# First MLP of a two-layer decoder: the relu turned by VectorE blocks and ScalarE quarter copies, modulation pieces issued on GpSimd's queue

## The chip, the core and the metric

The kernel runs on one core of a Trainium2 chip. The metric is device time in microseconds (us), lower is better. Besides the queues for transfers the core has TensorE (PE in the rows; PEld are its weight loads), VectorE (DVE), ScalarE (ACT), GpSimd (POOL) and SyncE (SP), which here only issues transfers. Each engine carries out its own instructions strictly in their order and waits on semaphores in that order.

## What is computed

Two decoder layers over 256 tokens with 2048 features, in float32. Cut to what matters here:

```python
for i in range(DEPTH):                      # 2 layers
    mod = (c_act @ w_ada[i] + b_ada[i])[:, None, :]
    sh_a, sc_a, g_a, sh_m, sc_m, g_m = jnp.split(mod, N_MOD, axis=-1)
    h = x * (1.0 + sc_a) + sh_a
    y = (diff_attention, sliding_window_attention)[i](h, ...)
    x = layer_norm(ALPHA * x + (1.0 + g_a) * y, ln_mix_g[i], ln_mix_b[i])
    h = x * (1.0 + sc_m) + sh_m
    y = jnp.square(jax.nn.relu(h @ w_up[i])) @ w_down[i]        # 2048 -> 8192 -> 2048
    x = layer_norm(ALPHA * x + (1.0 + g_m) * y, ln_mlp_g[i], ln_mlp_b[i])
```

The change concerns the squared-relu MLP of the first layer, and the loading of those parts of `w_ada` (the modulation weights) that are summed while this MLP runs.

## The kernel before

**Blocks.** Every large product is cut into blocks of 2048 input features by 512 output columns. A block's weights are four quarters of 1 MB (`raw`, five slots), each of two subtiles of 128x1024. ScalarE copies a subtile to `w_hi` in a shorter float format (`split_hi`, L528, six slots), VectorE subtracts (`split_lo`, L901) and writes the rest, `w_lo`, over `raw`. TensorE multiplies a subtile in twelve matmuls of 512 columns (L1709 to L1711): high by high, low by high, high by low, for two feature tiles and two token halves. So a block is 8 subtiles and 96 matmuls. ScalarE may be six subtiles ahead of TensorE, since `split_hi` waits for the slot (`used`).

**An MLP** has four rounds of eight blocks: four up blocks, each 512 columns of `h @ w_up`, then four down blocks, which multiply the 2048 squared columns by `w_down` and add to `y`. The loops over `b` in `mlp` are one block behind: at loop index b the engines split block b+1 and handle the result of block b between the subtiles (`before`, `later`, `hooks`; the number of a hook is the subtile after which it runs). With `i = b % 8`, the result is that of an up block for i from 0 to 3 and of a down block for i from 4 to 6. The text calls the block in which the result of an up block is handled a *turning block*; there are 16 in each MLP.

**Turning.** The result of an up block has tokens in partitions, and the down product needs features there. In the first layer ScalarE takes the relu out of PSUM into `R` (L553) after subtile 1 of the turning block, TensorE turns it by eight 128x128 transposes against the identity (`turn_up`, L1603) into PSUM, ScalarE squares it twice from there, once exactly and once into `f_hi` (L560, L561), and VectorE subtracts (`up_lo`, L1031) and gives `f_lo`. In the second layer (`ON_CHIP = (1,)`) TensorE takes no part: VectorE turns 16 pieces of 32x256 from SBUF to SBUF (L1040), which also moves each to its partitions, and ScalarE squares from there (L572, L573).

**Modulation pieces.** Beside this VectorE sums `c * w_ada` over 16 pieces of 128x1024 (512 KB) at a time (`ada_tile`, L929; the first of 16 is L926) in `ada_w`, which has four slots. In the first MLP these are 192 pieces, six or seven in each of the first 28 blocks, placed by `MLP_ADA` after subtiles 0, 1, 3, 5, 6, 7 and, where there are seven, 4. When 16 are summed, TensorE turns the sum (L1627, eight transposes) and VectorE reduces it (L960) after subtile 6. In the first four turning blocks VectorE also carries out the affine part of the layer norm (L1311, L1312) after subtile 7.

**Queues.** SP issues the transfers of weights and pieces in one written order: a quarter, then the pieces that belong to it. Each quarter waits until TensorE has used the one five before it, each piece until VectorE has added the one four before it. GpSimd clears `y` before the MLP (L1581) and has a few tiny power operations for the norms.

Of the kernel before, what the change touches and what calls it, by code (L numbers as in the profile page):

```python
# [21 lines left out]
KT = D // P  # L22
# [35 lines left out]

ON_CHIP = (1,)

# [43 lines left out]
UNIT_AT_B = {8 * (50 + i) + 3 + k: 8 * i + k for i in range(NCH) for k in range(8)}  # L104
MLP_HALVES = (12, 2)
MLP_GATE = (8, 0)
READY = 6
# [40 lines left out]
def trunk(nc, x_in, c_in, w_ada, b_ada, ln_mix_g, ln_mix_b, ln_mlp_g, ln_mlp_b, w_up, w_down,  # L148
          a_w_qkv, a_w_o, a_lambda_q1, a_lambda_k1, a_lambda_q2, a_lambda_k2, a_subln_g,
          b_w_qkv, b_b_qkv, b_sinks, b_w_o, b_b_o, ident_in, mask_in, rope_a_in, rope_b_in, out):  # L150
    with ExitStack() as ctx:
# [124 lines left out]
        ada_arrived = [sem(f"ada_arrived{i}") for i in range(ADA_SLOTS)]  # L276
        pre_arrived = [sem(f"pre_arrived{i}") for i in range(PRE_SLOTS)]
        ada_added = sem("ada_added")
        piece_taken = sem("piece_taken")
# [86 lines left out]
        def _(sp):  # L366
# [114 lines left out]
            def mlp(layer):  # L481
                def up(f, j):
                    col = f * D + j * NC
                    return lambda q: w_rows(w_up[layer], q * 4 * P, col)

                def down(f, j):
                    return lambda q: w_rows(w_down[layer], f * D + q * 4 * P, j * NC)

                load_block(up(0, 0))
                parts = [(1, 0), (1, 1), (1, 3), (1, 4), (0, 5), (1, 2)] if layer == 0 else [(1, 5)]  # L490
                tiles = iter([ada_src(l, part, half, kt) for l, part in parts for half in range(2) for kt in range(KT)])

                def of():
                    return next(tiles)

                for b in range(8 * QUARTERS - 1):
                    it, i = b // 8, b % 8
                    src = up(it, i + 1) if i < 3 else down(it, i - 3) if i < 7 else up(it + 1, 0)
                    load_block(src, mlp_pieces(b, 2 * len(parts)), of)

            mlp(0)

            for j in (4, 0, 1, 2, 3):
# [15 lines left out]
        def _(act):  # L519
# [35 lines left out]
            def up_square(j):  # L555

                def run():
                    act.wait_ge(t_full[0], st.t0.at(1))
                    wait(act, f_ready, st.up.at())
                    act.activation(SQ.rearrange("p t n -> p (t n)"), turn[:, 0], ACT.Square)  # L560
                    act.activation(f_hi[:, 4 * j:4 * j + 4], T[0], ACT.Square).then_inc(t_free[0], 1)  # L561
                    st.t0.n += 1
                    st.up.n += 1
                return run

# [229 lines left out]
            def mlp(layer, site, base):  # L795
# [3 lines left out]
                for b in range(8 * QUARTERS - 1):  # L799
# [5 lines left out]
                    if layer == 1 and b == 8 * QUARTERS - 3:  # L805
                        hk[0] = load_last_rows
                    if layer in ON_CHIP:
                        if i < 4:
                            hk[5] = up_square_there(i)
                        block_(before=up_relu if i < 4 else None, hooks=hk, at=2)  # L810
                        continue
# [75 lines left out]
        def _(dve):  # L887
# [31 lines left out]
            def ada_tile():  # L919
# [3 lines left out]
                src = ada_w[:, a.n % ADA_SLOTS]  # L923
                dve.wait_ge(ada_arrived[a.n % ADA_SLOTS], a.at(1 - PRE // ADA_SLOTS, 16, over=ADA_SLOTS))
                if kt == 0:
# [101 lines left out]
            def up_lo(i):  # L1027

                def run():
# [3 lines left out]
                    st.t0.n += 1  # L1033
                return run

            def up_turn_half(first):
# [417 lines left out]
            def mlp(layer, site, g):  # L1454
# [5 lines left out]
                for b in range(8 * QUARTERS - 1):  # L1460
# [11 lines left out]
                    if layer in ON_CHIP and i < 4:  # L1472
                        hooks[3] = up_turn_rest
                        block_(before=up_turn_across, later=(5, up_rest(i)), ada=mlp_pieces(b, halves), hooks=hooks)
                        continue
# [75 lines left out]
        def _(pool):  # L1551
# [21 lines left out]
            for u in range(UNITS_A):  # L1573
# [4 lines left out]
                power(sm[:, 7, 0:1], sm[:, 7, 1:2], orstd_ready)  # L1578
            site(1)
            pool.wait_ge(h_ready, 28)  # L1580
            pool.memset(y[:], 0.0).then_inc(y_clear, 1)  # L1581
            site(2)

# [527 lines left out]
```

## Time and profile before

| | us |
|---|---|
| median of 3 runs | 2228.59 |
| lowest and highest | 2226.88, 2228.90 |
| the profiled execution itself | 2228.67 |
| its span, first to last instruction | 2226.9 |

The profiled execution is within 0.1 us of the median, and 1.8 us of it lie outside the span. The mean granted clock of TensorE is 0.993 of full speed. In the rows below a time stands in us from the start of the span; a group of instructions has the number of them as xN, and the square bracket behind a row gives the idle time of the engine just before it and what ended that. Busy time of TensorE is modelled, and neighbouring matmuls overlap, so what an instruction costs there is read from the distance between starts.

### The profile page before, as it was taken

What the parts mean: (1) busy time and instruction counts of PE and PEld (TensorE: products, weight loads), DVE (VectorE), ACT (ScalarE), POOL (GpSimd) and SP (SyncE); (2) the same over time, 40 slices, a digit from 0 to 9 for tenths busy, and PEclk for the clock granted to TensorE, in tenths of its full rate; (3) what the DMA queues carried; (4) which work ended last, traced back from release to release, by engine and by line L of the source; (5) the groups of instructions that cost most, each with busy time, mean ns of one, the idle gap of its engine ahead of it and who ended that gap; (6) DMA issues with size and microseconds to landing.
All of it is one profiled execution on the core that took longest, in us unless ns stands there. A gap on an engine that the chain in (4) does not pass through costs nothing.

```text
span 2226.9 us, 26022 instructions
## 1 busy us (share of the span) xinstructions
PE 2168.5 (97%) x9952; PEld 1791.8 (80%) x9952; DVE 1790.6 (80%) x2057; ACT 981.3 (44%) x1330; POOL 33.4 (2%) x53
## 2 busy tenths in 40 slices
PE   6999999999999999999999999999999999999997
PEld 6887888877888888888888788777888888888886
DVE  6899998887997897888786888777966865874877
ACT  1135444546433443443353655536534443443441
POOL 0001000000000000000000000000000000000000
PEclk9899999999999999999999999999999999999999
DMA  9999888877999999999985643365766676666663
GB/s 360 384 331 347 322 320 300 306 245 256 361 364 325 354 366 335 325 380 350 323 311 190 198 152 119 122 207 190 236 221 223 213 241 206 219 217 219 228 234 113
DMA packets 262592, 596.41 MB, mean 268 GB/s; under 512 B 13426, under 2 KB 14788, under 8 KB 262468
## 3 DMA queue, kind: packets, MB, share of 16 engines
q1 hardware_dynamic: 254800, 579.45, 74.2%
q10 hardware_dynamic: 7668, 15.30, 2.2%
q8 instruction: 79, 1.29, 0.2%
q14 instruction: 45, 0.37, 0.0%
HBM read 592.60 MB, written 2.10 MB: 267 GB/s over the span
## 4 chain that ended last, share of the span: by engine, by line
PE 88%; DVE 7%; DMA 1%; issue 1%; ACT 1%; SPq 0%; DVEq 0%; POOL 0%; ACTq 0%; POOLq 0%
PE pair L1709 25%; PE pair L1711 25%; PE pair L1710 25%; DVE acc L916 2%; DVE w_lo L901 1%; PE pair L1967 1%; PE pair L1969 1%; PE pair L1968 1%; PE pair L1729 1%; PE pair L1731 1%; PE pair L1730 1%; PE turn L2041 1%; DMA y<-in_w_ada_dram 1%; PE turn L2022 1%; PE turn L1603 1%
## 5 line engine op out<-in xcount | busy, mean ns | idle before, releaser
L528 ACT ACTIVATE w_hi<-raw 128x1024 fp32r<-128x1024 f32 x712 | 726.8, 1056 | 620.2 <-PE pair L1711 297.4
L901 DVE TENSOR_TENSOR w_lo<-raw,w_hi 128x1024 fp32r<-128x1024 f32 x712 | 852.5, 1220 | 117.0 <-ACT w_hi L528 110.8
L1709 PE MATMUL pair<-w_hi,h_hi 128*128 128x512 f32 x1456 | 581.3, 399 | 1.5 <-DVE w_lo L901 0.8
L1711 PE MATMUL pair<-w_hi,h_lo 128*128 128x512 f32 x1456 | 567.8, 390 | 0.0
L1710 PE MATMUL pair<-w_lo,h_hi 128*128 128x512 f32 x1456 | 567.3, 390 | 0.0
L1709 PE MATMUL pair<-w_hi,f_hi 128*128 128x512 f32 x1056 | 414.0, 392 | 0.1
L1711 PE MATMUL pair<-w_hi,f_lo 128*128 128x512 f32 x1056 | 411.1, 389 | 0.0
L1710 PE MATMUL pair<-w_lo,f_hi 128*128 128x512 f32 x1056 | 410.9, 389 | 0.0
L929 DVE SCALAR_TENSOR_TENSOR acc<-ada_w,cvec,acc 128x1024 f32<-128x1024 f32 x300 | 383.6, 1279 | 1.8 <-DVE x L1312 0.9
L1709 PEld LDWEIGHTS pair<-w_hi,h_hi 128*128 128x128 f32 x1456 | 273.5, 188 | 62.9 <-DVE w_lo L901 6.3
L1711 PEld LDWEIGHTS pair<-w_hi,h_lo 128*128 128x128 f32 x1456 | 273.2, 188 | 58.4
L1710 PEld LDWEIGHTS pair<-w_lo,h_hi 128*128 128x128 f32 x1456 | 273.7, 188 | 55.5 <-issue 1.2
L1709 PEld LDWEIGHTS pair<-w_hi,f_hi 128*128 128x128 f32 x1056 | 198.2, 188 | 43.7 <-DVE w_lo L901 2.1
L1710 PEld LDWEIGHTS pair<-w_lo,f_hi 128*128 128x128 f32 x1056 | 198.3, 188 | 41.7 <-issue 1.0
L1711 PEld LDWEIGHTS pair<-w_hi,f_lo 128*128 128x128 f32 x1056 | 198.2, 188 | 41.5
L1040 DVE STREAM_TRANSPOSE work<-work 32x256 f32<-32x256 f32 x256 | 111.6, 436 | 55.7 <-ACT work L553 52.2
L553 ACT ACTIVATE work<-pair 128x1024 f32<-128x1024 f32 x32 | 32.9, 1029 | 222.3 <-PE pair L1711 222.3
L1066 DVE TENSOR_TENSOR y<-pair,y 128x1024 f32<-128x1024 f32 x30 | 36.7, 1224 | 101.2 <-PE pair L1711 101.2
L572 ACT ACTIVATE work<-work 128x1024 f32<-128x1024 f32 x16 | 17.0, 1062 | 90.7 <-DVE work L1040 90.7
L1967 PE MATMUL pair<-w_hi,f_hi 128*128 128x512 f32 x128 | 53.6, 419 | 1.9 <-DVE f_lo L1513 1.9
L1969 PE MATMUL pair<-w_hi,f_lo 128*128 128x512 f32 x128 | 50.1, 391 | 0.0
L1968 PE MATMUL pair<-w_lo,f_hi 128*128 128x512 f32 x128 | 49.9, 390 | 0.0
(190 smaller groups left out, 1669.5 us busy)
## 6 DMA issues: line engine op xcount, KB each, us to landing
ada_w<-in_w_ada_dram SPq DMA_DIRECT2D x320, 512.0 KB, 6.1
raw<-in_w_up_dram SPq DMA_DIRECT2D x128, 1024.0 KB, 6.1
raw<-in_w_down_dram SPq DMA_DIRECT2D x128, 1024.0 KB, 5.2
raw<-in_a_w_qkv_dram SPq DMA_DIRECT2D x48, 1024.0 KB, 7.6
ada_f<-in_w_ada_dram SPq DMA_DIRECT2D x44, 512.0 KB, 11.5
raw<-in_b_w_qkv_dram SPq DMA_DIRECT2D x20, 1024.0 KB, 5.2
raw<-in_a_w_o_dram SPq DMA_DIRECT2D x16, 1024.0 KB, 6.5
raw<-in_b_w_o_dram SPq DMA_DIRECT2D x16, 1024.0 KB, 5.1
```

What stands on the lines that cost most here:

```text
L528: act.activation(w_hi[:, (b.n * SUB + n) % SPLITS], raw[:, slot, k:k + 2], ACT.Copy).then_inc(hi_ready, 1)
L901: dve.tensor_tensor(w_lo[:, slot, k:k + 2], raw[:, slot, k:k + 2], w_hi[:, (b.n * SUB + n) % SPLITS].bitcast(F32), ALU.subtract).then_inc( ...
L916: ins = dve.scalar_tensor_tensor(dst, src, cvec[:, n % KT:n % KT + 1], dst, ALU.mult, ALU.add)
L929: ins = dve.scalar_tensor_tensor(acc[:, half], src, cvec[:, kt:kt + 1], acc[:, half], ALU.mult, ALU.add)
L1040: ins = dve.transpose(by_token(rows32(up_rows(RR), c), a), by_feature(rows32(up_rows(R), a), c))
L1066: dve.tensor_tensor(cols(y, j), pair[:, pp], cols(y, j), ALU.add).then_inc(evacuated, 1)
L1709: pe.matmul(o, hi[:, kt, at], w[:, k], start=kt == 0, stop=False)
L1710: pe.matmul(o, hi[:, kt, at], wl[:, k], start=False, stop=False)
L1711: mm = pe.matmul(o, lo[:, kt, at], w[:, k], start=False, stop=kt == KT - 1)
L1967: pe.matmul(o, f_hi[:, kt, at], w[:, k], start=kt == 0, stop=False)
L1968: pe.matmul(o, f_hi[:, kt, at], wl[:, k], start=False, stop=False)
L1969: mm = pe.matmul(o, f_lo[:, kt, at], w[:, k], start=False, stop=kt == KT - 1)
```

## The change

Four things change, all for the first MLP.

1. `ON_CHIP` becomes `(0, 1)` and `BY_SCALAR = (0,)` is added. TensorE no longer turns the relu of the first MLP. VectorE turns all of `R` in one instruction of 128x1024 in blocks of 32x32 into PSUM (`up_turn`), and ScalarE moves the blocks to their partitions by 16 copies of 32x256 out of PSUM into `RR` (`up_move`), eight after subtile 3 and eight after subtile 4 of the turning block.
2. The two squares come after subtile 5 and read `RR` in SBUF; the relu is taken after subtile 2 in place of 1; `f_lo` is made after subtile 5 in place of 4.
3. The 192 pieces of the first MLP are no longer issued by SP but by GpSimd, in a loop of its own, each with the same wait for the piece four before it. The first four are issued before `y` is cleared.
4. The pieces of that stretch have semaphores of their own (`pool_arrived`), and `ada_tile` picks which to wait for.

```diff
-ON_CHIP = (1,)
+ON_CHIP = (0, 1)
+BY_SCALAR = (0,)
+POOL_PIECES = MLP_HALVES[0] * KT
@@ SyncE
-                parts = [(1, 0), (1, 1), (1, 3), (1, 4), (0, 5), (1, 2)] if layer == 0 else [(1, 5)]
+                tiles = iter([ada_src(1, 5, half, kt) for half in range(2) for kt in range(KT)])
-                    load_block(src, mlp_pieces(b, 2 * len(parts)), of)
+                    load_block(src, mlp_pieces(b, MLP_HALVES[layer]) if layer == 1 else (), of)
@@ ScalarE
+            def up_move(first, last):
+                def run():
+                    act.wait_ge(up_blocks, st.turned.n + 1)
+                    for i in range(first, last):
+                        a, c = i // 4, i % 4
+                        ins = act.activation(by_token(rows32(up_rows(RR), c), a),
+                                             by_feature(rows32(turn[:, 0], a), c), ACT.Copy)
+                    if last == 16:
+                        ins.then_inc(up_moved, 1)
+                return run
@@ ScalarE, mlp
                     if layer in ON_CHIP:
+                        if i < 4 and layer in BY_SCALAR:
+                            hk[3], hk[4] = up_move(0, 8), up_move(8, 16)
@@ VectorE
+            def up_turn(b, pp):
+                dve.wait_ge(evacuated, b + 3)
+                dve.transpose(turn[:, 0], up_rows(R)).then_inc(up_blocks, 1)
@@ VectorE, mlp
-                        hooks[3] = up_turn_rest
-                        block_(before=up_turn_across, later=(5, up_rest(i)), ada=mlp_pieces(b, halves), hooks=hooks)
+                        if layer not in BY_SCALAR:
+                            hooks[3] = up_turn_rest
+                        block_(before=up_turn if layer in BY_SCALAR else up_turn_across, later=(5, up_rest(i)), ada=mlp_pieces(b, halves), hooks=hooks)
@@ GpSimd
             site(1)
+            def load_ada(n):
+                a = st.ada
+                for _ in range(n):
+                    pool.wait_ge(ada_added, a.at(1))
+                    pool.dma_start(ada_w[:, a.n % ADA_SLOTS], next(tiles)).then_inc(pool_arrived[a.n % ADA_SLOTS], 16)
+                    a.n += 1
+            load_ada(ADA_SLOTS)
             pool.wait_ge(h_ready, 28)
             pool.memset(y[:], 0.0).then_inc(y_clear, 1)
+            load_ada(POOL_PIECES - ADA_SLOTS)
             site(2)
```

ScalarE's queue in the first turning block of the first MLP, before (work is R, RR and the third of these buffers):

```order
L553 ACTIVATE work<-pair 128x1024
L528 ACTIVATE w_hi<-raw 128x1024 x3
L560 ACTIVATE work<-turn 128x1024
L561 ACTIVATE f_hi<-turn 128x1024
L528 ACTIVATE w_hi<-raw 128x1024 x5
```

The same place in the changed kernel:

```order
L556 ACTIVATE work<-pair 128x1024
L531 ACTIVATE w_hi<-raw 128x1024
L575 ACTIVATE work<-turn 32x2x4x32 x8
L531 ACTIVATE w_hi<-raw 128x1024
L575 ACTIVATE work<-turn 32x2x4x32 x8
L531 ACTIVATE w_hi<-raw 128x1024
L587 ACTIVATE work<-work 128x1024
L588 ACTIVATE f_hi<-work 128x1024
```

Between the relu and the squares there are now three splits with 16 copies between them, where there were three splits alone.

VectorE's queue from subtile 2 of a turning block in the second round, before:

```order
L901 TENSOR_TENSOR w_lo<-raw,w_hi 128x1024 x2
L929 SCALAR_TENSOR_TENSOR acc<-ada_w,cvec,acc 128x1024
L901 TENSOR_TENSOR w_lo<-raw,w_hi 128x1024
L1031 TENSOR_TENSOR f_lo<-work,f_hi 128x1024
L929 SCALAR_TENSOR_TENSOR acc<-ada_w,cvec,acc 128x1024
```

The same place in the changed kernel:

```order
L918 TENSOR_TENSOR w_lo<-raw,w_hi 128x1024
L1063 STREAM_TRANSPOSE turn<-work 128x1024
L918 TENSOR_TENSOR w_lo<-raw,w_hi 128x1024
L953 SCALAR_TENSOR_TENSOR acc<-ada_w,cvec,acc 128x1024
L918 TENSOR_TENSOR w_lo<-raw,w_hi 128x1024
L953 SCALAR_TENSOR_TENSOR acc<-ada_w,cvec,acc 128x1024
L918 TENSOR_TENSOR w_lo<-raw,w_hi 128x1024
L1086 TENSOR_TENSOR f_lo<-work,f_hi 128x1024
```

The transpose is new, between subtiles 2 and 3, and `f_lo` stands one subtile later.

GpSimd's queue from the norm ahead of the first MLP, before:

```order
L1561 TENSOR_TENSOR rstd<-rstd,minus_half 128x1 x2
L1581 MEMSET y 128x4096
L1561 TENSOR_TENSOR rstd<-rstd,minus_half 128x1 x2
L1586 MEMSET y 64x1024 x2
L1561 TENSOR_TENSOR rstd<-rstd,minus_half 128x1 x2
```

The same place in the changed kernel:

```order
L1591 TENSOR_TENSOR rstd<-rstd,minus_half 128x1 x2
L1619 DMA ada_w<-in_w_ada_dram 128x1024 x4
L1624 MEMSET y 128x4096
L1619 DMA ada_w<-in_w_ada_dram 128x1024 x188
L1591 TENSOR_TENSOR rstd<-rstd,minus_half 128x1 x2
```

The 192 transfers stand ahead of and behind the clearing of `y`; the power operations of the next norm come behind all of them.

## Rows read from the trace of the kernel before

**Rows 1.** The page: busy time and share of TensorE; chain by engine

```profile
PE 2168.5 (97%) x9952; PEld 1791.8 (80%) x9952; DVE 1790.6 (80%) x2057; ACT 981.3 (44%) x1330; POOL 33.4 (2%) x53
PE 88%; DVE 7%; DMA 1%; issue 1%; ACT 1%; SPq 0%; DVEq 0%; POOL 0%; ACTq 0%; POOLq 0%
```

**Rows 2.** Busy by stretch: PE, PEld, DVE, ACT, POOL, clock, DMA share, GB/s

```profile
524.00:1158.00 634.00, 634.00 (x2887) 525.37 (x2886) 535.72 (x470) 271.92 (x275) 0.00 (x0) 1.00 0.95 344
640.00:662.00 22.00, 22.00 (x103) 18.28 (x102) 20.94 (x20) 9.64 (x10) 0.00 (x0) 1.00 1.04 397
```

**Rows 3.** Timeline of TensorE around one turn: start, us, instruction

```profile
709.35 0.40 PE L1711 MATMUL pair<-w_hi,h_lo 128*128 128x512 f32 x1
709.58 1.04 PE L1603 MATMUL turn<-ident,work 128*128 128x128 f32 x8
710.38 0.47 PE L1709 MATMUL pair<-w_hi,h_hi 128*128 128x512 f32 x1
710.69 0.39 PE L1710 MATMUL pair<-w_lo,h_hi 128*128 128x512 f32 x1
```

**Rows 4.** Timeline of VectorE: two down blocks' results, each released by TensorE

```profile
659.92 1.22 DVE L1066 TENSOR_TENSOR y<-pair,y 128x1024 f32<-128x1024 f32 x1 [1.02 <-PE pair L1711]
...
681.68 1.23 DVE L1066 TENSOR_TENSOR y<-pair,y 128x1024 f32<-128x1024 f32 x1 [2.16 <-PE pair L1711]
```

**Rows 5.** Waits in the first MLP, 524 to 1158: us in all, times, longest

```profile
DVE w_lo L901 <- ACT w_hi L528: 47.4, 19, 6.8
ACT work L560 <- PE turn L1603: 37.4, 16, 2.5
DVE f_lo L1031 <- ACT f_hi L561: 25.2, 16, 1.6
```

**Rows 6.** Timeline of ScalarE at the start of a turning block

```profile
704.33 1.03 ACT L553 ACTIVATE work<-pair 128x1024 f32<-128x1024 f32 x1 [9.76 <-PE pair L1711]
705.26 2.94 ACT L528 ACTIVATE w_hi<-raw 128x1024 fp32r<-128x1024 f32 x3
```

**Rows 7.** Timeline of VectorE in the same block

```profile
712.63 1.23 DVE L1031 TENSOR_TENSOR f_lo<-work,f_hi 128x1024 fp32r<-128x1024 f32 x1 [1.60 <-ACT f_hi L561]
713.77 1.28 DVE L929 SCALAR_TENSOR_TENSOR acc<-ada_w,cvec,acc 128x1024 f32<-128x1024 f32 x1
714.97 1.22 DVE L901 TENSOR_TENSOR w_lo<-raw,w_hi 128x1024 fp32r<-128x1024 f32 x1
716.11 1.28 DVE L929 SCALAR_TENSOR_TENSOR acc<-ada_w,cvec,acc 128x1024 f32<-128x1024 f32 x1
```

**Rows 8.** Timeline of VectorE, second layer's turning by 32x256 pieces

```profile
1751.23 3.58 DVE L1040 STREAM_TRANSPOSE work<-work 32x256 f32<-32x256 f32 x8 [3.23 <-ACT work L553]
1754.82 1.23 DVE L901 TENSOR_TENSOR w_lo<-raw,w_hi 128x1024 fp32r<-128x1024 f32 x1
1756.08 3.59 DVE L1040 STREAM_TRANSPOSE work<-work 32x256 f32<-32x256 f32 x8
```

**Rows 9.** Timeline of ScalarE, second layer's attention: small copies out of PSUM

```profile
1306.89 0.38 ACT L855 ACTIVATE work<-turn 128x256 f32<-128x256 f32 x1 [0.94 <-PE turn L2031]
1307.17 0.37 ACT L860 ACTIVATE f_hi<-turn 64x256 fp32r<-64x256 f32 x1
1307.44 1.05 ACT L528 ACTIVATE w_hi<-raw 128x1024 fp32r<-128x1024 f32 x1
```

**Rows 10.** Timeline of ScalarE, second layer: the squares from SBUF

```profile
1781.77 1.06 ACT L572 ACTIVATE work<-work 128x1024 f32<-128x1024 f32 x1 [5.67 <-DVE work L1040]
...
1783.68 2.94 ACT L528 ACTIVATE w_hi<-raw 128x1024 fp32r<-128x1024 f32 x3
```

**Rows 11.** Timeline of VectorE: the affine part after subtile 7, first round

```profile
585.15 1.21 DVE L1311 TENSOR_TENSOR x<-x,bc 128x1024 f32<-128x1024 f32 x1
...
587.83 1.28 DVE L929 SCALAR_TENSOR_TENSOR acc<-ada_w,cvec,acc 128x1024 f32<-128x1024 f32 x1 [0.21 <-DVE x L1312]
```

**Rows 12.** The issues of pieces by SP (L374): time to landing

```profile
DMA to landing us min/median/max: 3.4/6.1/14.3
```

**Rows 13.** Groups of VectorE in the first MLP, 524 to 1158: busy us, mean ns

```profile
L960 DVE TENSOR_REDUCE mod<-turn 128x8 f32<-128x1024 f32 x8 | 9.8, 1220 | 1.8 <-PE turn L1627 1.8
L926 DVE TENSOR_SCALAR acc<-ada_w,cvec 128x1024 f32<-128x1024 f32 x11 | 8.2, 749 | 0.0
```

More of the change, by code:

```diff
@@ L277, in trunk @@
         pre_arrived = [sem(f"pre_arrived{i}") for i in range(PRE_SLOTS)]
+        pool_arrived = [sem(f"pool_arrived{i}") for i in range(ADA_SLOTS)]
         ada_added = sem("ada_added")
@@ L489, in mlp @@
                 load_block(up(0, 0))
-                parts = [(1, 0), (1, 1), (1, 3), (1, 4), (0, 5), (1, 2)] if layer == 0 else [(1, 5)]
-                tiles = iter([ada_src(l, part, half, kt) for l, part in parts for half in range(2) for kt in range(KT)])
+                tiles = iter([ada_src(1, 5, half, kt) for half in range(2) for kt in range(KT)])
                 def of():
@@ L498, in mlp @@
                     src = up(it, i + 1) if i < 3 else down(it, i - 3) if i < 7 else up(it + 1, 0)
-                    load_block(src, mlp_pieces(b, 2 * len(parts)), of)
+                    load_block(src, mlp_pieces(b, MLP_HALVES[layer]) if layer == 1 else (), of)
             mlp(0)
+            st.ada.n += POOL_PIECES
             for j in (4, 0, 1, 2, 3):
@@ L923, in ada_tile @@
                 src = ada_w[:, a.n % ADA_SLOTS]
-                dve.wait_ge(ada_arrived[a.n % ADA_SLOTS], a.at(1 - PRE // ADA_SLOTS, 16, over=ADA_SLOTS))
+                turns = (a.n - PRE) // ADA_SLOTS + 1
+                before = 3 * 2 * KT // ADA_SLOTS
+                if turns <= before:
+                    dve.wait_ge(ada_arrived[a.n % ADA_SLOTS], 16 * turns)
+                elif turns <= before + POOL_PIECES // ADA_SLOTS:
+                    dve.wait_ge(pool_arrived[a.n % ADA_SLOTS], 16 * (turns - before))
+                else:
+                    dve.wait_ge(ada_arrived[a.n % ADA_SLOTS], 16 * (turns - POOL_PIECES // ADA_SLOTS))
                 if kt == 0:
@@ L1579, in _ @@
             site(1)
+            parts = [(1, 0), (1, 1), (1, 3), (1, 4), (0, 5), (1, 2)]
+            tiles = iter([ada_src(l, part, half, kt) for l, part in parts for half in range(2) for kt in range(KT)])
+            st.ada.n = PRE + 3 * 2 * KT
+            def load_ada(n):
[5 more added lines that the diff above has]
+            load_ada(ADA_SLOTS)
             pool.wait_ge(h_ready, 28)
             pool.memset(y[:], 0.0).then_inc(y_clear, 1)
+            load_ada(POOL_PIECES - ADA_SLOTS)
             site(2)
```

## Prediction

> **What bounds the kernel now.** I read the page first: TensorE is busy for 97% of the span and holds 88% of the chain that ended last [rows 1]. Then the stretch of the first MLP, 524 to 1158 us: TensorE is busy for all 634 us of it at full clock, while VectorE is busy for 535.7 (84%), ScalarE for 271.9 (43%), and the transfer queues for 0.95 of their time at 344 GB/s [rows 2]. So there TensorE alone sets the pace, and whatever leaves its queue is won, as long as nobody else falls behind. The second thing to see is how little is free beside it: in one stretch of this MLP the transfers run at 397 GB/s with a share of 1.04 and VectorE is busy for 20.9 of 22 us [rows 2]. Last I read the waits. VectorE's own in this MLP are 47.4 us for ScalarE's splits and 25.2 us, 1.6 in each of 16 blocks, for the squares [rows 5]: that is its reserve, and it stands at fixed places in its queue.
>
> **What is removed.** A matmul of 512 columns follows the next at 0.227 us: the distance of two down results without any turn is 681.68 − 659.92 = 21.76 us for 96 of them [rows 4]. Around a turn the starts go 709.35, then 710.38 and 710.69 [rows 3]; that is 1.34 us for two steps of 0.227, so a turn costs 0.89. Sixteen go: **−14.2 us**. This is the whole possible gain, for the other work of TensorE stays.
>
> **What ScalarE gets.** A 128x256 copy from PSUM is followed by the next instruction after 0.28 us, a 64x256 copy after 0.27 [rows 9]. The change's copies have 256 elements in 32 partitions; I take 0.28, the row with the same type and an SBUF target. Eight are 2.24 us, 16 are 4.5. With eight splits at 0.945 (2.94 for three that overlap by their ends, [rows 6]), the relu (0.93, same rows) and the two squares (1783.68 − 1781.77 = 1.91, [rows 10]) ScalarE has 14.9 of 21.76 us: it fits by load. What counts is the latency from relu to squares.
>
> **What VectorE gets.** Sixteen transposes of 128x1024 into PSUM are not in the trace. From below: 32x256 takes 3.58/8 = 0.45 us [rows 8], so four times the columns cost at least what a subtraction of 128x1024 does, 1.22. From above: if the time went with partitions too, the 16 pieces of 32x256, 7.2 us. I take 1.24: 0.45 plus 768 more columns at the rate of VectorE's other operations (1.04 ns a column, from 1.22 us for 1024 against 0.45 for 256). Such a transpose doesn't overlap with its neighbours: the split ahead of it takes 1.26 instead of 1.14 (1754.82 to 1756.08, [rows 8]). So 1.36 us more in VectorE's queue in each turning block.
>
> **The new loop.** I carry one turning block on. Let X be the start of VectorE's transpose. It ends at X+1.24; with 0.04 for the semaphore ScalarE copies until 3.52, splits subtile 4 until 4.47, copies until 6.71, splits subtile 5 until 7.66, squares until 9.57 (its last end 9.67). VectorE idles for this (it has splits 4 and 5 and two pieces in the meantime) and then does f_lo (1.14, [rows 7]), a piece (1.20) and split 6 (1.14): the split ends at X+13.3. Four pairs of piece and split (2.34 each, [rows 7]) lead to the next transpose, at X+22.6. TensorE's block is 21.76. **The loop through both engines is 0.84 us longer than TensorE's block**, where before each block began afresh at TensorE's turn, which both engines waited for [rows 5].
>
> At the start of a round X is 1.26 us after TensorE's end of the up block: 0.20 to the relu, which lasts 1.03 [rows 6], and 0.03. TensorE wants subtile 6 at 6×2.72 = 16.3, split 6 ends at 14.5: 1.75 of reserve. A round has three such steps to the fourth turning block: 3×0.84 − 1.75 = 0.8 us of stall. A mod sum after subtile 6 costs VectorE 1.35 (1.22 [rows 13] and a small operation) and TensorE 0.89, so 0.46 more where it falls in a turning block before the last. For rounds 2, 3 and 4: 1.3 + 0.8 + 0.7 = **2.8 us**. In the down blocks VectorE wins back some 3 us a block.
>
> The first round has the affine part too: 587.83 − 585.15 = 2.68 us in each of four blocks [rows 11]. The loop is 25.3, 3.5 over TensorE's 21.76. Before, TensorE just escaped, since the turn gave VectorE 0.89 more and the loop was shorter by the copies and the transpose. Now the stalls are 3.5 − 1.75 = 1.8 in the second block, 3.5 and 3.5 in the third and fourth, and about 2.3 in the first down block, for the fourth affine part: **11.1 us**.
>
> Sum: −14.2 + 2.8 + 11.1 = −0.3 us. With copies at 0.265 the same working gives some 10.5 us of stalls, so −3.7; I put the forecast between the two rows, at −1.5. From the profiled execution's 2228.67: 2227.2, and since that is 0.1 from the median, **2227 us**. Copies at 0.30 give +5, at 0.35 +18, a transpose 0.1 longer +1.8 (each microsecond in the loop counts in some 14 of 16 blocks).
>
> **The pieces.** SP loses 192 issues, and its quarters no longer stand behind a piece's wait. That is worth nothing to TensorE, which never waited in this MLP; it gives ScalarE its weights earlier. GpSimd issues a piece when the one four before it has been added. In a dense run (after 6, 7, 0, 1) VectorE is back at that slot after three pairs and a split, 3×2.34 + 1.14 = 8.2 us; the landing takes 6.1 us in the median and up to 14.3 when it is queued behind quarters [rows 12]. In a queue of its own it stands behind no quarter, but shares the engines. Bounds: 0 if it stays under 8.2, and what one rival below gives if not. The memset of `y` isn't late: the four issues before it wait for pieces added before the norm. The power operations for the next norm stand behind the last piece, which is added three blocks before they are needed. Beside this SP's and ScalarE's queues are unchanged but for the order shown.
>
> VectorE's L926, at 749 ns against 1.28 us for any other piece of the same size, is in a faster form [rows 7, 13]. The Trainium skill, "SBUF — State Buffer" (the box on the DVE blocks DMA trap), says that a transfer issued from GpSimd has its descriptors written by that engine's cores, which are locked out while VectorE runs in a two-port fast mode, and tells one to issue from SP or ACT. By that rule at most 12 issues of 192 could meet an L926, 0.75 us each, inside the reserve of 2.1 us; the sum stays as it is. No row here shows an issue from GpSimd.
>
> **Rivals.**
> *The loop is shorter than I think (faster).* It decides at 0.23 us a copy, where the loop is down to TensorE's 21.76 and only the first round stalls. The bare columns of a copy are 0.22 us (0.945 for 1024 columns less 0.28 for 256, [rows 6, 9], is 0.87 ns each); at that the first round has 2.5 over, so 2.5 − 1.75, 2.5, 2.5 and 2.2, 8 us, and the time is 2222. If moreover VectorE didn't stop for ScalarE there, its load alone would count: 8×1.14 + 6.9×1.20 + 1.36 + 1.14 + 2.68 = 22.5, only 0.8 over 21.76, 3 us in four blocks, and 2217. Against: the small copies of [rows 9] have a fixed part, and [rows 5] show that VectorE does stop at the squares.
> *Pieces land late (slower).* It decides at 8.2 us from the slot's release. VectorE stands before the piece, and behind it in its queue are the splits TensorE needs. At 9 us the wait of 0.8 enters the loop about once a turning block, with half of it again elsewhere: some +7, so 2234; at 10 us +15 to +17, so 2243. For: the queues are at 0.95 already, and the turning blocks now ask for the same bytes in 21.76 us instead of 22.65. Against: the median of 6.1.
> The Trainium skill, "DMA: Bandwidth & Descriptors" (Specifications), gives about 1 us to the first byte from GpSimd's path and 0.6 from the other. By that the landing would be at 6.5, an estimate from that page and the median, still under the limit.
> *Quarter copies cost more (slower).* Their access is in runs of 32 elements with a stride. It decides at 0.29 us a copy; at 0.30 to 0.35 the time is 2233 to 2246. For: no such form is in the trace. Against: VectorE's pieces with the same pattern run at the usual rate [rows 8].
> *The change doesn't do what it says.* If TensorE's block stayed at 22.65 because something else needs that long (the transfers: 7.8 MB in 21.76 us are 358 GB/s), no stall and no gain: 2229. The 397 GB/s of [rows 2] speak against it.
>
> **How the numbers follow.** The loop as worked out, 2223 to 2231: 0.45, the likeliest, 2227. Shorter loop, 2217 to 2222: 0.14. Late pieces, 2232 to 2245: 0.20. Slow copies, 2233 to 2246: 0.14. Transfers as the bound, 2229: 0.07. A difference under 0.2%, 4.5 us, can't be told from none. Faster by more: 0.14 and 0.08 of the first case, 0.22. Slower by more: 0.34 and 0.01 of the first, 0.35. Within: 0.43. The range takes in the bounds of the copy's and the landing's cost and part of the short loop: 2219 to 2245.
>
> **What would show it.** TensorE without L1603, and blocks of 21.76 us in the later rounds; gaps of TensorE that end at VectorE's w_lo, 10 us or more in the first four turning blocks and about 1 us in each later round; the copies at 0.28 and the transpose at 1.24. ScalarE waiting for the transpose 0.3 us in the first turning block of a round and for longer in each next one. VectorE waiting for pieces before L953 would show the second rival; copies over 0.29 the third; stalls of 8 us or less in the first round, with the copies under 0.23, the first rival. I am wrong if the time is outside 2223 to 2231, and wrong in the mechanism if the stalls aren't mostly in the first round.

## The result and the profile after

| | before | after |
|---|---|---|
| median of three runs, us | 2228.59 | 2256.65 |
| lowest and highest, us | 2226.88, 2228.90 | 2255.18, 2257.93 |
| the profiled execution's span, us | 2226.9 | 2253.4 |

The changed kernel takes 1.0129 of the time of the kernel before (95% interval 1.0114 to 1.0143): 28.1 us more. The forecast was 2227 us with a range up to 2245, so it was wrong in size, and the change is a clear loss where I had given the largest chance, 0.43, to no difference. This section reads where the time went; the experiments then name the cause.

The page first, busy time by engine and the chain that ended last by engine; these answer to [rows 1]:

```profile
PE 2162.2 (96%) x9824; PEld 1772.6 (79%) x9824; DVE 1810.1 (80%) x2073; ACT 1081.2 (48%) x1586; POOL 137.1 (6%) x245
PE 71%; DVE 15%; ACT 7%; issue 6%; DMA 1%; SPq 0%; ACTq 0%; POOL 0%; DVEq 0%; POOLq 0%
```

TensorE has 128 instructions less, as it should, but its part of the chain fell from 88% to 71%, and VectorE (15%), ScalarE (7%) and the time that the profile can't name (issue, 6%) took it. Something other than TensorE sets the pace in a part of the program. Which part, the stretches tell. Each row below is one round's four turning blocks in the kernel after, from the first matmul of the first block to the first matmul of the down block behind them (columns as in [rows 2]):

```profile
521.80:628.64 106.84, 92.03 (x393) 71.71 (x391) 86.21 (x76) 70.01 (x111) 14.03 (x26) 1.00 0.86 296
717.64:814.13 96.49, 90.30 (x393) 72.24 (x392) 77.15 (x68) 68.95 (x110) 14.06 (x27) 1.00 0.91 320
902.99:999.87 96.88, 91.21 (x402) 73.06 (x401) 77.49 (x69) 68.97 (x110) 14.02 (x26) 1.00 0.92 327
1088.67:1184.70 96.03, 90.63 (x390) 72.38 (x388) 77.05 (x66) 68.98 (x110) 11.86 (x22) 1.00 0.87 306
```

And the same stretches of the kernel before:

```profile
523.70:615.27 91.57, 91.57 (x425) 76.22 (x424) 81.69 (x72) 44.75 (x46) 0.00 (x0) 1.00 0.93 331
704.13:795.74 91.61, 91.61 (x425) 76.22 (x424) 75.97 (x67) 44.63 (x46) 0.00 (x0) 1.00 0.91 326
884.60:977.10 92.50, 92.50 (x433) 77.05 (x432) 76.31 (x68) 44.74 (x46) 0.00 (x0) 1.00 0.95 339
1065.91:1158.36 92.45, 92.45 (x422) 76.14 (x421) 74.53 (x64) 45.84 (x47) 0.00 (x0) 1.00 0.91 324
```

The four rounds are 15.3, 4.9, 4.4 and 3.6 us longer, 28.1 in all, and the down blocks behind them are as long as before but for 0.1. So the whole loss sits in the sixteen blocks that the change touches, and more than half of it in the first round. (The profiled spans differ by 26.5 only, since this execution enters the stretch at 521.80 in place of 523.70. That start also lies at 524.66 in run 1 and at 523.35 in run 8 below; why is not shown.) TensorE runs at the full granted clock (1.00) in all of them; it only stands still: 92.03 busy of 106.84. The transfers' share fell to 0.86 to 0.92: they aren't the brake.

Who made TensorE wait? The waits of the kernel after in the same MLP, 524 to 1190 us (in all, times, longest):

```profile
DVE w_lo L918 <- ACT w_hi L531: 62.9, 33, 3.0
PEld pair L1753 <- DVE w_lo L918: 47.0, 36, 2.8
ACT work L575 <- DVE turn L1063: 42.1, 16, 5.4
PE pair L1753 <- DVE w_lo L918: 31.8, 29, 2.4
DVE f_lo L1086 <- ACT f_hi L588: 10.7, 16, 0.7
```

TensorE waits 29 times for VectorE's low parts of the weights, where it waited not once before. VectorE waits for ScalarE's high parts 33 times, twice in each of the sixteen blocks and once more. And ScalarE waits for VectorE's transpose (longest 5.4). It is the loop through both engines that the prediction had drawn, and it is longer than the prediction made it. ScalarE's timeline in one turning block shows by what:

```profile
720.20 3.07 ACT L575 ACTIVATE work<-turn 32x256 f32<-32x256 f32 x8 [0.38 <-DVE turn L1063]
723.28 1.06 ACT L531 ACTIVATE w_hi<-raw 128x1024 fp32r<-128x1024 f32 x1
724.36 3.10 ACT L575 ACTIVATE work<-turn 32x256 f32<-32x256 f32 x8
727.49 1.06 ACT L531 ACTIVATE w_hi<-raw 128x1024 fp32r<-128x1024 f32 x1
```

Eight copies last from 720.20 to 723.28, 0.385 us each from start to start, where [rows 9] gave 0.28. And the group of all of them on the page:

```profile
L575 ACT ACTIVATE work<-turn 32x256 f32<-32x256 f32 x256 | 96.1, 375 | 45.1 <-DVE turn L1063 42.1
```

A copy alone takes 375 ns, as the 128x256 copy of [rows 9] does with its 0.38. What is missing is the overlap: there the next instruction starts 0.1 us before the copy's end, here only after it. VectorE's timeline in the same block and at the start of the next:

```profile
718.90 1.26 DVE L1063 STREAM_TRANSPOSE turn<-work 128x1024 f32<-128x1024 f32 x1 [3.92 <-ACT work L556]
720.07 1.20 DVE L918 TENSOR_TENSOR w_lo<-raw,w_hi 128x1024 fp32r<-128x1024 f32 x1
...
724.37 1.22 DVE L918 TENSOR_TENSOR w_lo<-raw,w_hi 128x1024 fp32r<-128x1024 f32 x1 [1.92 <-ACT w_hi L531]
...
728.58 1.23 DVE L918 TENSOR_TENSOR w_lo<-raw,w_hi 128x1024 fp32r<-128x1024 f32 x1 [1.79 <-ACT w_hi L531]
730.47 1.23 DVE L1086 TENSOR_TENSOR f_lo<-work,f_hi 128x1024 fp32r<-128x1024 f32 x1 [0.67 <-ACT f_hi L588]
...
742.14 1.22 DVE L918 TENSOR_TENSOR w_lo<-raw,w_hi 128x1024 fp32r<-128x1024 f32 x1
743.28 1.25 DVE L1063 STREAM_TRANSPOSE turn<-work 128x1024 f32<-128x1024 f32 x1
```

From transpose to transpose 743.28 − 718.90 = 24.4 us, where the prediction had 22.6 and TensorE's block is 21.76. Behind each group of eight copies stands a split that VectorE waits for. Last the pieces on GpSimd: their issues and the time from issue to landing.

```profile
L1619 POOL DMA_DIRECT2D ada_w<-in_w_ada_dram x192 | 103.7, 540 | 549.2 <-DVE acc L953 529.0
DMA to landing us min/median/max: 3.8/6.5/9.0
```

### The profile page after: what moved, and what is told of

The parts are those of the page before. It is cut to its first block, busy times and chain, and to the rows that moved or that the text cites. A ratio compares the mean times of both kernels' runs of the same rounds, so it can differ in the third digit from the quotient of the medians.

```text
span 2253.4 us, 26022 instructions
## 1 busy us (share of the span) xinstructions
PE 2162.2 (96%) x9824; PEld 1772.6 (79%) x9824; DVE 1810.1 (80%) x2073; ACT 1081.2 (48%) x1586; POOL 137.1 (6%) x245
## 4 chain that ended last, share of the span: by engine, by line
PE 71%; DVE 15%; ACT 7%; issue 6%; DMA 1%; SPq 0%; ACTq 0%; POOL 0%; DVEq 0%; POOLq 0%
PE pair L1753 20%; PE pair L1755 20%; PE pair L1754 20%; DVE acc L953 4%; ACT work L575 3%; DVE w_lo L918 3%; DVE acc L933 2%; PE pair L2011 1%; PE pair L2013 1%; PE pair L2012 1%; PE pair L1773 1%; ACT w_hi L531 1%; DMA ada_f<-in_w_ada_dram 1%; PE pair L1775 1%; PE pair L1774 1%
## 5 line engine op out<-in xcount | busy, mean ns | idle before, releaser
L1753 PE MATMUL pair<-w_hi,f_hi 128*128 128x512 f32 x1056 | 414.9, 393 | 12.4 <-DVE w_lo L918 12.4
L1754 PE MATMUL pair<-w_lo,f_hi 128*128 128x512 f32 x1056 | 411.1, 389 | 0.0
L1755 PE MATMUL pair<-w_hi,f_lo 128*128 128x512 f32 x1056 | 411.1, 389 | 0.0
L1619 POOL DMA_DIRECT2D ada_w<-in_w_ada_dram x192 | 103.7, 540 | 549.2 <-DVE acc L953 529.0
L575 ACT ACTIVATE work<-turn 32x256 f32<-32x256 f32 x256 | 96.1, 375 | 45.1 <-DVE turn L1063 42.1
L587 ACT ACTIVATE work<-work 128x1024 f32<-128x1024 f32 x32 | 33.7, 1052 | 90.7 <-DVE work L1069 90.7
L1591 POOL TENSOR_TENSOR rstd<-rstd,minus_half 128x1 f32<-128x1 f32 x8 | 4.7, 591 | 1096.6 <-DVE rstd L1194 1096.6
```

The source lines that it names most:

```text
L575: ins = act.activation(by_token(rows32(up_rows(RR), c), a), by_feature(rows32(turn[:, 0], a), c), ACT.Copy)
L587: act.activation(SQ.rearrange("p t n -> p (t n)"), up_rows(RR), ACT.Square)
L1619: pool.dma_start(ada_w[:, a.n % ADA_SLOTS], next(tiles)).then_inc(pool_arrived[a.n % ADA_SLOTS], 16)
L1753: pe.matmul(o, hi[:, kt, at], w[:, k], start=kt == 0, stop=False)
L1754: pe.matmul(o, hi[:, kt, at], wl[:, k], start=False, stop=False)
L1755: mm = pe.matmul(o, lo[:, kt, at], w[:, k], start=False, stop=kt == KT - 1)
```

## The experiments

The theories at the start: the copies' latency in the loop costs the time (A), or the pieces' new queue does (B); and, as the copies are slow, what makes them so. A short diff stands with each run; lines are those of the changed kernel. All times are medians, and the kernel before, run beside them on the same chip, took 2227.9 to 2228.8 us.

**1. The pieces back on SP's queue.** The change's other half alone.

```diff
 # on SP, in mlp(layer)
-load_block(src, mlp_pieces(b, MLP_HALVES[layer]) if layer == 1 else (), of)
+load_block(src, mlp_pieces(b, MLP_HALVES[layer]), of)
 # on GpSimd
-load_ada(ADA_SLOTS)
-load_ada(POOL_PIECES - ADA_SLOTS)
```

VectorE waits on the semaphores of SP's pieces again.

> The change with the 192 pieces issued by SP again, in the old order; the turning by VectorE and ScalarE stays. Theory A (the loop through the copies costs everything, the queue nothing): within 4 us of the changed kernel, so 24 to 32 us over the kernel before, with the copies at 0.385 us from start to start. Theory B (pieces issued by GpSimd cost time: their landing, or VectorE held up by it): at least 8 us faster than the changed kernel.

Measured: 2258.61 us, 1.0136 of before (1.0121 to 1.0151). The blocks are the same as in the kernel after, to a tenth of a microsecond. The queue has no part in the loss.

**2. GpSimd's queue alone**, with the turn on TensorE as before.

```diff
-ON_CHIP = (0, 1)
-BY_SCALAR = (0,)
+ON_CHIP = (1,)
+BY_SCALAR = ()
```

> The other part alone: GpSimd issues the pieces, and TensorE turns the relu as before. Theory A: no difference to the kernel before, within 3 us. Theory B: slower than the kernel before by 8 us or more.

Measured: 2227.51 us, 0.9998 (0.9989 to 1.0007). Theory B is out from both sides: the change splits into a part that costs nothing and one that costs it all.

**3. Every second copy left out.** Half of the turned relu then holds old data; all else stands.

```diff
-for i in range(first, last):
+for i in range(first, last, 2):
```

> The changed kernel with every second of the 16 copies left out (four and four stay), so half of the turned relu is stale; nothing else is changed. Theory A: the loop is 8 x 0.385 = 3.1 us shorter, under TensorE's block outside the first round; carrying the steps on gives some 5 us of stalls, all in the first round, and 9 us less than the kernel before (2219). Rival (VectorE's load or the transfers bound the turning blocks, the copies are beside that): less than 10 us gained against the changed kernel, so over 2245.

Measured: 2221.07 us, 0.9969 (0.9957 to 0.9980), 35.6 us under the kernel after for 128 copies less. Eight copies of 0.387 are 3.1 us a block, and sixteen blocks would be worth 49.5; the rest of them had no stall left to take. Theory A had 2219 us with some 5 us of stalls left, the rival over 2245. TensorE's waits in this kernel, of the same stretch:

```profile
PEld pair L1753 <- DVE w_lo L918: 7.3, 5, 2.8
PE pair L1753 <- DVE w_lo L918: 5.1, 3, 2.3
```

What is left stands in the first round: its blocks are 21.76, 23.12, 23.98 and 25.67 us, the turning blocks of the later rounds 21.76 or, with a mod sum, 22.65 or 22.69 (one has two mod sums and 23.53). So the copies' time is the cause, not the transfers and not VectorE's load, and TensorE's blocks do get as short as the turn's removal promised. Whether the copies cost by their load on ScalarE or by where they stand in its queue, this run can't tell; run 7 does.

**4. What is slow about the copies.** One kernel in which the sixteen turning blocks use eleven forms of copy in turn (most of them compute another thing than the turned relu).

```diff
-ins = act.activation(by_token(rows32(D, c), a), by_feature(rows32(S, a), c), ACT.Copy)
+# L584: by_token(rows32(D, a), c), by_feature(rows32(S, a), c)    same partitions in and out
+# L587: part(rows32(D, c), a, 256), part(rows32(S, a), c, 256)    straight runs, shifted
+# L604: by_token(D, c), by_feature(S, c)                          128 partitions, four copies
+# L607: part(rows32(D, 1), c, 256), part(rows32(S, 0), c, 256)    always from quarter 0 to quarter 1
+# and others: straight and unshifted, 64 partitions, 512 and 128 elements
```

> The changed kernel, in which each turning block of the first MLP makes its copies out of PSUM in one of eleven forms (quarter copies as they are; not shifted to other partitions; in straight runs of 256; 4 copies of 32x256, 64x256 and 128x256; 8 of 32x512 and of 128x128), so the turned relu is wrong. Read is the distance from start to start. Theory P (a copy of 32 partitions doesn't overlap with the next one, whatever else): 0.385 for all with 32 partitions, 0.28 for 64 and 128. Theory S (the shift to other partitions does it): 0.385 only where input and output partitions differ. Theory R (runs of 32 elements do it): 0.28 wherever the runs are straight.

Measured, ScalarE's timeline at four of the forms; the splits around them are in 128 partitions:

```profile
526.51 3.07 ACT L581 ACTIVATE work<-turn 32x256 f32<-32x256 f32 x8 [0.53 <-DVE turn L1101]
529.60 1.06 ACT L531 ACTIVATE w_hi<-raw 128x1024 fp32r<-128x1024 f32 x1
...
553.58 2.36 ACT L584 ACTIVATE work<-turn 32x256 f32<-32x256 f32 x8 [5.43 <-DVE turn L1101]
555.95 1.06 ACT L531 ACTIVATE w_hi<-raw 128x1024 fp32r<-128x1024 f32 x1
...
719.34 1.06 ACT L531 ACTIVATE w_hi<-raw 128x1024 fp32r<-128x1024 f32 x1 [0.38 <-DVE turn L1101]
720.31 1.15 ACT L595 ACTIVATE work<-turn 32x256 f32<-32x256 f32 x4
721.36 1.05 ACT L531 ACTIVATE w_hi<-raw 128x1024 fp32r<-128x1024 f32 x1
...
896.17 1.07 ACT L531 ACTIVATE w_hi<-raw 128x1024 fp32r<-128x1024 f32 x1 [0.38 <-DVE turn L1101]
897.26 1.17 ACT L607 ACTIVATE work<-turn 32x256 f32<-32x256 f32 x4
898.45 1.06 ACT L531 ACTIVATE w_hi<-raw 128x1024 fp32r<-128x1024 f32 x1
```

The distances within each form, read between all its copies (a quarter is 32 partitions, quarter 0 starts at partition 0, and so on):

| line | form | from copy to copy, us |
|---|---|---|
| L581 | the change's own: each copy writes another quarter | 0.38 to 0.39 |
| L587 | the same, in straight runs of 256 | 0.38 to 0.39 |
| L584, L590 | same quarter in and out, four copies each | 0.26 to 0.29, and 0.38 where the quarter changes |
| L595 | always quarter 0 | 0.26 |
| L607 | always from quarter 0 to quarter 1 | 0.26 to 0.28 |
| L598, L601, L604 | 64 and 128 partitions | 0.26 |

All three theories written down for this run fall as they were stated. It isn't the small count of partitions (L595 has 32 and 0.26), not the runs of 32 elements (L587 has none and is slow, L604 has them and is fast), and not the shift from one quarter to another (L607 shifts). What the slow ones share is that the next copy is in another place. The seams tell which property of the place it is. Around L595, in the partitions 0 to 31, a split in all 128 precedes by 720.31 − 719.34 = 0.97 us and follows after the usual 0.26 (721.36 − 720.31 = 1.05 for four): the set of partitions changes there, and nothing is lost. Around L607, which writes from partition 32 on, the same two are 1.09 and 0.387. The times read as one rule: **a ScalarE instruction of these forms starts some 0.12 us earlier, before the end of the one ahead of it, if it starts in the same partition, and only after that end if the first partition changes.** It is read from first partitions 0, 32, 64 and 96, the only ones here. The kernel of the forms was timed once, at 2232.48 us; as it mixes them, that time isn't used.

With this rule in hand, the kernel before turns out to have shown it. The two rows of [rows 9] are a 128x256 copy and a 64x256 one from partition 0 on. Two units later the same lines work on the upper half, L860 on the partitions 64 to 127:

```profile
1316.25 0.38 ACT L855 ACTIVATE work<-turn 128x256 f32<-128x256 f32 x1
1316.66 0.38 ACT L860 ACTIVATE f_hi<-turn 64x256 fp32r<-64x256 f32 x1
1317.06 1.06 ACT L528 ACTIVATE w_hi<-raw 128x1024 fp32r<-128x1024 f32 x1
```

0.41 and 0.40 us instead of 0.28 and 0.27. Of the 32 of L860, 26 have a split behind them: it starts after 0.26 us in the 10 on the lower half and after 0.40 or 0.41 in the 16 on the upper.

**5. The same sixteen copies in another order**, to see whether only the written side counts. Four in a row now write the same quarter and read four different ones; in the change it is the other way round.

```diff
-a, c = i // 4, i % 4
+a, c = i % 4, i // 4
```

> The changed kernel with its sixteen quarter copies in another order: the same sixteen source and destination quarters, but the feature block c counts in the outer loop and the token block a in the inner, so four copies in a row write the same 32 partitions and each reads other ones. (As the changed kernel stands, four in a row read the same 32 partitions and each writes other ones, at 0.387 us start to start.) Theory Out (the overlap of two ScalarE instructions goes when the second writes other partitions than the first): three of four copies start 0.265 us after the one before and the fourth 0.386, 0.295 in the mean; the prediction's own steps with 0.295 in the place of 0.28 give the turned loop stalls of some 16 us against 40 and a time 2 to 3 us over the kernel before, 2231 us (range 2228 to 2234). Rival Either (it goes when the partitions of either side change): every copy at 0.387 as in the changed kernel, and 2256 to 2257 us.

Measured: 2256.66 us, 1.0131 (1.0116 to 1.0147), and the copies at 0.387 as before (one eight of them and the split behind):

```profile
722.00 3.10 ACT L575 ACTIVATE work<-turn 32x256 f32<-32x256 f32 x8 [0.38 <-DVE turn L1063]
725.11 1.06 ACT L531 ACTIVATE w_hi<-raw 128x1024 fp32r<-128x1024 f32 x1
```

The rival holds and the theory that only the written side counts falls (it had 0.295 us and 2231): a change on either side is enough, the read or the written one. A copy is named by its source quarter a and its destination quarter c, and no two have both in common, so no order of the sixteen keeps both sides fixed: 0.387 is the price of the change's idea, not of its order.

**6. The affine parts moved to the down blocks** (b = 4 to 7), where VectorE has time; the copies stay.

```diff
-if b < NCH:
-    hooks[7] = affine(site, b)
+first = 4 if layer == 0 else 0
+if first <= b < first + NCH:
+    hooks[7] = affine(site, b - first)
```

ScalarE's loads of the rows that the last two parts need stand four blocks later too, after subtile 7 in place of 6.

> The changed kernel with the four affine parts of the first MLP (2.68 us each on VectorE) moved from the four turning blocks of the first round to the four blocks behind them. Theory A (both engines form a loop, and what is in it is added): the stalls of the first round fall from 4.9 + 5.1 + 5.2 + 2.3 to 2.2 + 2.4 + 2.5, so 10 us less than the changed kernel, 15 to 18 over the kernel before. Rival (the first round is bound by transfers): under 4 us gained.

Measured: 2246.51 us, 1.0079 (1.0064 to 1.0094): 10.1 under the kernel after, still 17.7 over before. The first round's blocks are now 22.22, 24.37, 24.37 and 25.37 us, like those of any other round. The affine part made the first round worse; the loop alone is too long everywhere.

**7. The splits ahead of the copies.** On ScalarE splits 3 to 6 stand ahead of all copies and both squares, on VectorE f_lo stands behind piece 6. The copies are as slow as before; only nobody waits behind them for weights.

```diff
-hk[3], hk[4] = up_move(0, 8), up_move(8, 16)
-if i < 4:
-    hk[5] = up_square_there(i)
+hk[6] = moved_and_squared(i)      # up_move(0, 16), then the squares
 # on VectorE
-block_(before=up_turn, later=(5, up_rest(i)), ...)
+block_(before=up_turn, after=(6, up_rest(i)), ...)
```

ScalarE's loads of the norm's rows, in two blocks, stand after subtile 7 in place of 6. The order of both engines is altered at once, so what each alone is worth stays open.

> The changed kernel with ScalarE's order in the turning block altered: splits 3 to 6 ahead of all 16 copies and the squares, and f_lo after the piece that follows subtile 6 on VectorE. The same instructions as the changed kernel. Theory A (latency in the loop, not load): VectorE no longer waits for splits behind copies, and the loop falls under TensorE's block; carried on step by step there is 0.6 us of stall, and the time is 13 us below the kernel before (2215). Rival (the load of ScalarE or VectorE is too high with copies at 0.385): still slower than the kernel before.

Measured: 2217.96 us, 0.9954 (0.9937 to 0.9970): 38.7 under the kernel after and 10.8 under before, 3 us above the 2215 on record. The group of copies and the waits of TensorE for VectorE in the same stretch:

```profile
L575 ACT ACTIVATE work<-turn 32x256 f32<-32x256 f32 x256 | 95.9, 375 | 3.8 <-DVE turn L1072 1.0
```

```profile
DVE f_lo L1095 <- ACT f_hi L588: 24.2, 11, 3.8
PE pair L1765 <- DVE w_lo L925: 0.7, 1, 0.7
PE pair L1765 <- DVE f_lo L1095: 0.2, 1, 0.2
```

The copies take 95.9 us as before (375 ns each), and TensorE waits 0.9 us instead of 31.8 (by the starts of blocks, against run 8 below, 1.9 us of stalls instead of 42.7). So it isn't the load of ScalarE or VectorE that cost the time, but the order: two splits stood behind the copies and a third behind the squares, and VectorE stopped for the two and for the squares in each turning block.

**8. Both: 6 and 7.**

> e6 and e5 together: splits first, and the affine parts in the down blocks of the first round. Theory A: no stall in the first MLP, 14 us below the kernel before (2214 to 2216).

Measured: **2214.94 us, 0.9937 (0.9923 to 0.9952)**, faster than both kernels. The page's chain, and the turning blocks of the first two rounds with the sum over all four:

```profile
PE 87%; DVE 9%; issue 1%; ACT 1%; DMA 1%; ACTq 0%; DVEq 0%; POOL 0%; SPq 0%; POOLq 0%
```

```profile
523.35:611.29 87.94, 87.94 (x394) 72.90 (x392) 80.25 (x71) 68.57 (x110) 15.11 (x28) 1.00 0.97 349
700.15:788.11 87.96, 87.96 (x393) 72.90 (x392) 79.69 (x71) 68.28 (x110) 15.09 (x28) 1.00 0.99 356
...
sum 353.57, PE 353.57 PEld 292.36 DVE 316.95 ACT 273.65 POOL 56.65; mean PE 88.39 PEld 73.09 DVE 79.24 ACT 68.41 POOL 14.16
```

TensorE is busy for all of it (PE 353.57 of 353.57 us). The four stretches are 353.6 us, against 368.1 of the kernel before: 14.6 less, the turn's whole price. Against them the kernel after has 42.7 us of stalls (396.24 − 353.57, the sums of the four stretches, both by the starts of blocks; the 31.8 us of its waits is less because a matmul's modelled end reaches into the gap).

The same with the copies in the order of 5 tells whether ScalarE's time still counts there:

> The kernel of e7_splits_first_affine (weight splits ahead of the copies and squares, affine parts with the down blocks) with the quarter copies in the order of e9_columns_outer. In e7 no turning block stalled, so ScalarE's time is not on the path: both theories expect the time of e7, 2214 to 2216 us, whether a copy takes 0.295 or 0.387. A time under 2213 would say that the copies still cost something there; one over 2217 that the order disturbs another thing.

Measured: 2214.89 us, 0.9939 (0.9926 to 0.9951). Nothing changes, but as 5 left the copies at 0.387 this run says only that their order is free.

**9. The best version with the pieces on SP.** The edit of 1 on the kernel of 8.

> e7 with the pieces issued by SP in the old order. Theory A: the queue makes no difference, within 3 us of e7. Rival: without the turn the transfers have less time per block, and quarters that stand behind a piece's wait come late; then e8 is slower than e7 by 4 us or more.

Measured: 2221.30 us, 0.9965 (0.9952 to 0.9978): 6.4 us more than with GpSimd's queue (the profiled execution is the slowest of five, 2223.04; the fastest took 2216.72). The theory on record, within 3 us, is missed, and its rival, 4 us or more, holds. ScalarE in the last turning block of the second round, and the waits of the stretch:

```profile
775.66 1.07 ACT L531 ACTIVATE w_hi<-raw 128x1024 fp32r<-128x1024 f32 x1 [4.20 <-DMA raw<-in_w_down_dram]
776.63 6.17 ACT L575 ACTIVATE work<-turn 32x256 f32<-32x256 f32 x16
```

```profile
ACT w_hi L531 <- DMA raw<-in_w_down_dram: 107.4, 35, 5.1
ACT w_hi L531 <- DMA raw<-in_w_up_dram: 80.1, 30, 6.4
DVE f_lo L1089 <- ACT f_hi L588: 44.2, 16, 4.8
PE pair L1758 <- DVE f_lo L1089: 7.3, 3, 2.6
```

Here ScalarE waits 187.5 us for the weights' transfers; in run 8 it is 121.3, by the same two groups. With the splits in front, a transfer that comes 4.2 us late holds back the copies, the squares and f_lo, and in three of the rounds TensorE needs f_lo before it is there (7.3 us in three waits, about the difference). The queue of GpSimd is worth at most 2 us in the kernel after (2258.61 in run 1 against 2256.65, with intervals that overlap) and 6 us once the loop is gone. That the weights are late because they stand behind pieces in SP's queue is inferred: the bytes are the same and only the issuing queue differs.

## Why the prediction was wrong

**The turn gone from TensorE, −14.2 us: right.** The blocks of run 8 are shorter by 14.6 in all, and no L1603 is left.

**The copies, 0.28 us each: the step that failed.** I took the 128x256 row of [rows 9] as the nearest and said so; the count of elements and the type were right, and a copy's own 375 ns is that row's 0.38. What I carried over with it was the overlap of 0.1 us, and in runs 4 and 5 that has a condition that the row met and the change's copies don't: the next instruction starts in the same partition. The view held the answer. I read the first unit that I found, at 1307 us, where both lines start in partition 0; at 1316 us the same lines stand 0.41 and 0.40 apart (run 4). Measured 0.387, that is 16 × 0.107 = 1.7 us more in each loop. And the split ahead of the second eight, which start at partition 64, loses its own overlap: 1.08 (723.28 to 724.36) instead of 0.945, 0.1 more. The loop is then 22.6 + 1.7 + 0.1 = 24.4, as measured.

**The reserve, 1.75 us: gone by the same term.** Split 6 ended at X+13.3 in my working. It stands behind both groups of copies, so it ends 1.8 later, and TensorE is reached at once, in the first turning block of each round (22.02 us in the second, against 21.76) instead of the fourth. Three loops of 2.6 over TensorE's 21.76 plus this first one are 7.9 us and a mod sum's 0.46, some 8.4 a round, where I had 1.3, 0.8 and 0.7.

| round | stalls foreseen | measured, against run 8 |
|---|---|---|
| first, with its down block | 11.1 | 19.0 |
| second | 1.3 | 8.5 |
| third | 0.8 | 8.0 |
| fourth | 0.7 | 7.2 |

The same working, carried on block by block with 0.387 instead of 0.28, gives some 40 us of stalls, the figure on record for run 5, so 26 us over the kernel before; measured 42.7 and 28.1. The structure was right: the loop through both engines, the first round worst by the affine part (run 6), ScalarE's wait for the transpose short in a round's first block (0.4 to 0.5 us) and longer behind it (2.2 to 5.4). But by the prediction's own sign, that the stalls are mostly in the first round, its picture fails too: they are 19.0 of 42.7 us, since the loop that was to be nearly harmless in the later rounds costs some 8 us in each.

**The transpose, 1.24 us: right in itself** (1254 ns in the mean), wrong in that I denied it an overlap. The next instruction starts 1.17 after it (718.90 to 720.07) and it starts 1.14 after the one before (742.14 to 743.28), so it costs 1.17 and not 1.36 in the queue. The loop's sum above had its length alone, and so that is no part of the error there.

**The pieces, nothing: right for this kernel.** They land after 6.5 us in the median against my limit of 8.2 (9.0 at most), and VectorE waited 1.9 us for them in all. The rival of late pieces, to which I gave 0.20, is out by runs 1 and 2. The landing of 6.5 us that I had estimated from the Trainium skill, "DMA: Bandwidth & Descriptors" (Specifications: about 1 us to the first byte on GpSimd's path, 0.6 on the other), agrees with the trace of this kernel. The lock-out of GpSimd's descriptor writing that the Trainium skill, "SBUF — State Buffer" (the box on the DVE blocks DMA trap), describes costs nothing that these runs show: run 2 is at 0.9998, with the longest of 192 issues at 715 ns against 540 in the median. Only a dozen of VectorE's additions there, those like L926, are in the faster form, so the rule was hardly put to the test.

**The rival of slow copies: the right term for the wrong reason, with a chance of only 0.14 and too low a top.** Its list ended at 0.35 and 2246; carried on to 0.387 at its own 2.6 us for each 0.01 it would have read 2255. I drew it from the pattern of 32-element runs, which has no part in it, and held VectorE's pieces of [rows 8] against it. The bound should have been worked out from the row at hand: 0.38 is the copy's own length in [rows 9], so no overlap at all was the natural upper end of the copy's cost, and by it the range would have reached 2254, still 3 us short.

**The transfers as the bound: out.** In run 8 the turning blocks run at 21.76 us with a share up to 0.99.

## What to carry to other kernels

Where an operation is cut into many small ones, read the distance to the next over all instances of the nearest line, not one, and ask what differs where it isn't the same; the full length of one, with no overlap, belongs into the upper bound. When a load is moved to an idle engine, its place in that engine's queue can count as much as its length: ahead of the splits that others wait for, 96 us of copies went with 42.7 us of stalls, and behind them the same copies with 1.9 (run 7). A loop that runs through two engines must be shorter than the bound engine's period, and its excess is paid in each pass; what needn't stand in it (the affine part here, 10.1 us in run 6) belongs outside.

## What the runs showed of the hardware

- In these kernels ScalarE starts an instruction about 0.12 us earlier, before the end of the one ahead, if both sides start in the same partition as in that one (0.26 to 0.29 us from start to start for 256 elements, in 32, 64 or 128 partitions alike, shifted or not), and not if the first partition changes on the input or on the output side (0.387). It shows in runs 4 and 5 and in L860 of the kernel before (0.26 against 0.40). The Trainium skill, "ScalarE: Activation LUTs" (What ACT_TABLE_LOAD costs), says that ACTIVATEs in a row overlap by about 93 ns. That agrees with the 0.1 us of [rows 9], but not with the change's copies, which don't overlap; here the measurement decides.
- 512 elements take 0.48 to 0.50 us from copy to copy where the quarter stays and 0.58 to 0.59 where it changes (run 4), so the loss doesn't grow with the elements.
- A transpose by 32x32 blocks of 128x1024 float32 elements from SBUF into PSUM takes VectorE 1.25 us, about as much as a subtraction of the same size (1.22): 2.9 times the 436 ns of a 32x256 piece for 16 times its elements.
- A 512 KB transfer issued by GpSimd keeps it busy for 0.54 us and lands 6.5 us later in the median in the kernel after (332 GB/s in all from 524 to 1158 us) and 7.0 in run 8, where SP's land after 6.1 in the kernel before [rows 12] (344 GB/s).
